# Banded attention: five units turned by VectorE and DMAs instead of TensorE

## The reference, cut to what matters

```python
def window_attention(q, k, v, sink):      # 8 heads, 2 groups of 4 heads share k and v
    scores = einsum('bnqgrd,bnkgd->bngrqk', qb, kb) * HEAD_DIM ** -0.5   # per block of 128
    scores = where(mask, scores + bias, -inf)      # three neighbouring key blocks, |t-s| <= 128
    m = maximum(max(scores, -1), sink)
    p = exp(scores - m)
    probs = p / (sum(p, -1) + exp(sink - m))
    out = einsum('bngrqk,bnkgd->bnqgrd', probs, vb)
ya = window_attention(...) * silu(ga)
```

## Time and profile before

| what | before |
|---|---|
| median of 3 runs | 610.73 us (609.9 to 611.62) |
| profiled execution | 610.19 us, span 608.4 us |
| granted clock of TensorE, mean | 0.997 |
| TensorE busy | 597.4 us, 98% |
| VectorE, ScalarE, GpSimd busy | 446.7, 357.1, 293.3 us |

### The profile page before, as it was taken

One profiled execution on the slowest core, in us unless ns is written; L12 is line 12 of the kernel. 1 busy time (PEld: TensorE's weight loads), 2 busy tenths in 40 slices (PEclk: granted clock), 3 DMA queues, 4 the chain that ended last, 5 costly groups with the idle time before them and its releaser, 6 DMA issues.

```text
span 608.4 us, 9184 instructions
## 1 busy us (share of the span) xinstructions
PE 597.4 (98%) x3076; PEld 482.6 (79%) x3076; DVE 446.7 (73%) x802; ACT 357.1 (59%) x762; POOL 293.3 (48%) x273
## 2 busy tenths in 40 slices
PE   8999999999999999999999999999999999999996
PEld 7888888888888888888887777767776777888885
DVE  4776753334434439889999788988998988799884
ACT  5644243213333238777886777878887789534563
POOL 4510704315756432536537545876876766510601
PEclk9999999999999999999999999999999999999998
DMA  6688458674876620101015967767767745598042
GB/s 222 207 256 245 146 163 266 202 270 135 256 263 233 201 67 1 36 1 36 2 27 137 250 150 183 188 165 194 194 161 195 183 133 182 176 387 319 1 170 108
DMA packets 72431, 102.11 MB, mean 168 GB/s; under 512 B 10232, under 2 KB 43008, under 8 KB 72384
## 3 DMA queue, kind: packets, MB, share of 16 engines
q1 hardware_dynamic: 72224, 101.25, 55.7%
q10 hardware_dynamic: 160, 0.27, 0.1%
HBM read 60.17 MB, written 31.62 MB: 151 GB/s over the span
## 4 chain that ended last, share of the span: by engine, by line
PE 78%; DMA 7%; DVE 5%; ACT 4%; SPq 3%; POOL 2%; issue 1%; ACTq 0%
PE ps L1821 18%; PE ps L1823 18%; PE ps L1822 18%; PE ps L2093 4%; DMA p_land<-probs_scratch 4%; PE ps L1993 3%; PE ps L2112 2%; PE ps L2113 2%; PE ps L2023 2%; SPq L628 2%; PE ps L2003 2%; DMA probs_scratch<-p_blk 2%; PE ps L2028 2%; PE ps L1980 2%; PE ps L1979 2%; DVE pT_lo L1671 2%
## 5 line engine op out<-in xcount | busy, mean ns | idle before, releaser
L1671 DVE TENSOR_TENSOR pT_lo<-ps,pT_hi 128x512 fp32r<-128x512 f32 x102 | 68.8, 688 | 25.0 <-ACT pT_hi L1234 24.9
L1821 PE MATMUL ps<-hT_hi,w_hi 128*128 128x512 f32 x208 | 84.0, 404 | 0.0
L1221 ACT ACTIVATE p_b<-ps,stat 128x1024 f32<-128x1024 f32 x64 | 71.4, 1116 | 19.2 <-DVE stat L1646 18.9
L1823 PE MATMUL ps<-hT_hi,w_lo 128*128 128x512 f32 x208 | 81.3, 391 | 0.0
L1822 PE MATMUL ps<-hT_lo,w_hi 128*128 128x512 f32 x208 | 81.0, 389 | 0.0
L1646 DVE TENSOR_REDUCE stat<-ps 128x1 f32<-128x1024 f32 x64 | 76.6, 1215 | 2.2 <-PE ps L2043 2.0
L1234 ACT ACTIVATE pT_hi<-ps 128x512 fp32r<-128x512 f32 x102 | 60.0, 596 | 18.8 <-PE ps L2093 18.5
L2093 PEld LDWEIGHTS ps<-ident,p_b 128*128 128x128 f32 x408 | 47.9, 140 | 19.6 <-DVE pT_lo L1671 5.4
L2093 PE MATMUL ps<-ident,p_b 128*128 128x128 f32 x408 | 62.6, 276 | 0.5 <-DVE pT_lo L1671 0.3
L2112 PE MATMUL ps<-pT_hi,vB 128*128 128x512 f32 x128 | 54.8, 428 | 1.5 <-POOL pT_lo L925 1.5
L809 POOL TENSOR_SCALAR p_w<-p_w,stat 128x384 f32<-128x384 f32 (+1 forms) x40 | 24.4, 623 | 55.5 <-DVE stat L1554 55.5
(11 more groups left out here) (222 smaller groups left out, 1487.7 us busy)
## 6 DMA issues: line engine op xcount, KB each, us to landing
w_raw<-w_in SPq DMA_DIRECT2D x13, 512.0 KB, 4.3
probs_scratch<-p_blk SPq DMA_DIRECT2D x52, 128.0 KB, 2.8
p_land<-probs_scratch SPq DMA_DIRECT2D x13, 512.0 KB, 4.6
x_in<-x SPq DMA_DIRECT2D x8, 512.0 KB, 4.1
wt_raw<-w_out SPq DMA_DIRECT2D x8, 512.0 KB, 4.5
t_scratch<-wt_hi SPq DMA_DIRECT2D x16, 256.0 KB, 2.5
t_scratch<-wt_lo SPq DMA_DIRECT2D x16, 256.0 KB, 2.8
q<-q_h SPq DMA_DIRECT2D x16, 256.0 KB, 3.6
```

The source lines that it names most:

```text
L1221: nc.scalar.activation(p_b[:, (U + 1) % 4, :], ps[:, b:b + 2, :].rearrange("p b c -> p (b c)"), ACT.Exp, bias=nm_b[:, U % 4:U % 4 + 1], ac ...
L1671: nc.vector.tensor_tensor(pT_lo[at_], ps[:, 4 + a, :].rearrange("p (k c) -> p k c", c=P), f(pT_hi[at_]), ALU.subtract).then_inc(s_bTl, 1)
L1821: nc.tensor.matmul(o, a_hi, b_hi, start=first, stop=False, skip_group_check=goes_on)
L1823: return nc.tensor.matmul(o, a_lo, b_hi, start=False, stop=last, skip_group_check=goes_on)
```

## The change

Units 5, 7, 9, 11 and 13, all with g = 1 and three key blocks, take the way through DRAM. After GpSimd has multiplied all four heads of such a unit, VectorE turns 32x32 blocks of all 1536 columns in step u+1 into `w_blk`, four stores of 192 KB and one load of 768 KB follow on SyncE's queue, and in step u+3 ScalarE copies the high part from `w_land`, GpSimd subtracts (three times, one per key block) and TensorE multiplies with the values. Both strips lie in parts of `q_st` whose queries are done. The other units stay as they were. So step 6 has no products, steps 8, 10, 12 and 14 have those of units 5, 7, 9 and 11 and no transposes, step 16 has those of 13 ahead of 15. The gated groups are dealt out anew: 2 and 6 in steps 5 and 6, then 3 in odd and 5 in even steps up to 14.

The diff, cut to its core (semaphore counts that shift by the number of routed units are left out):

```diff
+W_ROUTED = [5, 7, 9, 11, 13]
+POOL_HEADS = [3, 2, 2] + [2 if u in ACT_UNITS else 4 if u in W_ROUTED else 3 for u in range(3, 16)]
+        w_strips = at("w_strips", 65, [P, 4, 2, SEQ])
@@ beside
+            cut = 2 if s in (5, 6) else 3 if 7 <= s <= 14 else 4
+            return N_WIN_JOB + (s + 1) // 2, range(cut) if s % 2 else range(cut, KT)
+        def w_now(s):
+            return [u for u in (s - 3, s - 1) if 0 <= u < W_UNITS and (u in W_ROUTED) == (u == s - 3)]
+        w_blk, w_land = (w_strips[:, :, i, 0:3 * P] for i in range(2))
@@ SyncE
+            def store_w_probs(u):
+                i = W_ROUTED.index(u)
+                sp.wait_ge(s_pblk, NT + i + 1)
+                for q in range(4):
+                    sp.dma_start(pw_scr[i % 2, :, :, q, :].rearrange("a p c -> p a c"),
+                                 w_blk[q * Q32:(q + 1) * Q32]).then_inc(s_psto, 16)
+            def fetch_w_probs(u):
+                i = W_ROUTED.index(u)
+                sp.wait_ge(s_psto, 64 * (NT + i + 1))
+                if i >= 1:
+                    sp.wait_ge(s_plo, NT + 3 * i)
+                sp.dma_start(w_land, pw_scr[i % 2].rearrange("a p q c -> (a p) q c")).then_inc(s_pin, 16)
+            store_w_probs(5)
+            fetch_w_probs(5)
             sp.wait_ge(s_wr, NM - 1)
...
             load_k(0)
+            for u in (7, 9, 11):
+                store_w_probs(u)
+                fetch_w_probs(u)
             sp.wait_ge(s_wr, NM)
             load_q(0)
+            store_w_probs(13)
+            fetch_w_probs(13)
@@ GpSimd
+            def routed_w_lo(u, i):
+                c = W_FIRST[u] + i
+                pool.wait_ge(s_wTh, c + 1)
+                nc.gpsimd.tensor_tensor(w_quads_out(pT_wl[:, c % 2, :]), w_quads(i), w_quads_out(f(pT_wh[:, c % 2, :])),
+                                        ALU.subtract).then_inc(s_plo, 1)
@@ head0_hi
+                pool.wait_ge(s_psto, 64 * (NT + WR))
                 nc.gpsimd.tensor_scalar(k_1[:, 0, :], k_raw[:, :], 1.0, 1.0, ALU.mult, ALU.mult).then_inc(s_h0kh, 1)
@@ its loop over steps
+                for u in w_now(s):
+                    if u in W_ROUTED:
+                        for i in range(3):
+                            routed_w_lo(u, i)
                 if s < W_UNITS:
                     probs_w(s)
-                if s >= 2:
-                    gate_w(s - 2)
+                for u in w_now(s - 1):
+                    gate_w(u)
@@ ScalarE, pT_w_hi
+                if u in W_ROUTED:
+                    act.wait_ge(s_pin, 16 * (NT // 2 + W_ROUTED.index(u) + 1))
...
+                    nc.scalar.activation(w_quads_out(pT_wh[:, c % 2, :]), w_quads(i), ACT.Copy).then_inc(s_wTh, 1)
@@ VectorE
+            def turn_w_probs(u):
+                i = W_ROUTED.index(u)
+                dve.wait_ge(s_wp, sum(POOL_HEADS[:u + 1]))
+                dve.wait_ge(s_ws, REP * 6)
+                if i >= 1:
+                    dve.wait_ge(s_psto, 64 * (NT + i))
+                nc.vector.transpose(w_blk.rearrange("p a (k c) -> p a k c", c=Q32),
+                                    p_w[:, u % 2, :, :].rearrange("p r (i a c) -> p a (r i) c", a=4, c=Q32)) \
+                    .then_inc(s_pblk, 1)
@@ its loop over steps, ahead of recip_w(s)
+                if s - 1 in W_ROUTED:
+                    turn_w_probs(s - 1)
@@ TensorE, pv_w
-                pe.wait_ge(s_wTl, c + 1)
+                if u in W_ROUTED:
+                    pe.wait_ge(s_plo, NT + 3 * W_ROUTED.index(u) + i + 1)
+                else:
+                    pe.wait_ge(s_wTl, W_TURN[u] + i + 1)
@@ its loop over steps
+                for v in now[:-1]:
+                    pv_w(v, 0)
+                    gated(g, ks[:1])
+                    pv_w(v, 1)
+                    gated(g, ks[1:2])
+                    pv_w(v, 2)
+                    ks = ks[2:]
+                if u not in W_ROUTED:
+                    for i in range(min(n, 2)):
+                        turn_w(u, i)
```

More of the change, by code:

```diff
@@ L66 @@
 ACT_UNITS = range(2, 16, 2)
-POOL_HEADS = [3, 2, 2] + [2 if u in ACT_UNITS else 3 for u in range(3, 16)]
+W_ROUTED = [5, 7, 9, 11, 13]
+WR = len(W_ROUTED)
+POOL_HEADS = [3, 2, 2] + [2 if u in ACT_UNITS else 4 if u in W_ROUTED else 3 for u in range(3, 16)]
 SLOPE = [2.0 ** -(h + 1) for h in range(HEADS)]
@@ L1179, in _ @@
             for s in range(W_UNITS + 1):
-                keys = range(W_FIRST[s - 1], W_FIRST[s]) if s >= 1 else []
+                now = w_now(s)
+                keys = [(now[-1], i) for i in range(len(w_keys(now[-1])))] if now else []
                 live = s < W_UNITS
-                if s >= 2:
-                    o_w_lo(s - 2)
+                for u in w_now(s - 1):
+                    o_w_lo(u)
+                for u in now[:-1]:
+                    for i in range(len(w_keys(u))):
+                        pT_w_hi(u, i)
                 if live:
@@ L1187, in _ @@
                     first_v_hi()
+                for u in now[:-1]:
+                    o_w_lo(u)
                 for i, c in enumerate(keys[:2]):
-                    pT_w_hi(c)
+                    pT_w_hi(*c)
                     if live:
@@ L1556, in probs_w @@
             def probs_w(u):
+                if POOL_HEADS[u] == REP:
+                    return
                 dve.wait_ge(s_wrd, u + 1)
@@ L1606, in _ @@
             for s in range(W_UNITS + 1):
-                keys = range(W_FIRST[s - 1], W_FIRST[s]) if s >= 1 else []
+                now = w_now(s)
+                keys = [(u, i) for u in now if u not in W_ROUTED for i in range(len(w_keys(u)))]
                 live = s < W_UNITS
@@ L1616, in _ @@
                     head0_lo()
-                if s >= 1:
-                    pT_w_lo(keys[0])
+                for u in now[:-1]:
+                    o_w_sum(u)
+                for c in keys[:1]:
+                    pT_w_lo(*c)
                 if live:
@@ L1983, in turn_w @@
             def turn_w(u, i):
-                c = W_FIRST[u] + i
+                c = W_TURN[u] + i
                 if i == 0:
                     pe.wait_ge(s_wp, sum(POOL_HEADS[:u + 1]))
-                    pe.wait_ge(s_wpd, u + 1)
+                    pe.wait_ge(s_wpd, sum(v not in W_ROUTED for v in range(u + 1)))
                     if u in ACT_UNITS:
@@ L2050, in _ @@
                 g, ks = beside(s)
[L2051 removed]
+                now = w_now(s)
+                u = now[-1] if now else None
+                n = len(w_keys(u)) if now else 0
                 if s < W_UNITS:
                     scores_w(s)
[L2054 to L2058 removed]
+                for v in now[:-1]:
[8 more added lines that the diff above has]
+                        turn_w(u, i)
                 if 2 <= s < W_UNITS or s == 0:
```

109 lines of the change are left out of this document (60 added, 49 removed).

## The result

| | before | after |
|---|---|---|
| median | 611.17 us (609.9 to 612.16, 4 runs) | 630.03 us (629.8 to 631.15, 4 runs) |
| ratio | | 1.0328, interval 1.0297 to 1.0359 |
| profiled span | 608.4 us | 628.0 us |
| granted clock, mean | 0.997 | 0.986 |
| TensorE busy, matmuls | 597.4 us, 3076 | 598.4 us, 3016 |

The changed kernel takes 630.03 us, 3.3% more than before, where 632 us were forecast. TensorE has 60 matmuls less and is busy no less, since some of them run at half clock. First the page of the profile after: busy time by engine, then TensorE and its granted clock in 40 slices. They answer to the earlier trace rows.

A forecast was written before the change was run, and what follows sets the result against it. TensorE, busy 98% of the span, was taken as the bound. Even steps 9.3, steps 6 and 7 -0.2, step 16 8.0 and clock 4.4 gave 21.5 us more, so 632 us, range 619 to 641.

The forecast's parts named there:

- Removed transposes: TensorE, five routed units: 1.37 us less work per unit, 6.8 us in all, the most that can be won.
- rival 1: Window stage: transposes are won and all waits covered, 604 us; chance 4%.
- Even steps: Steps 8, 10, 12, 14: TensorE waits for GpSimd's queued subtractions; longer by 2.7, 2.4, 3.4, 0.8, together 9.3 us.
- Odd steps and steps 6 and 7: Odd steps stay at 7.17 us on VectorE's chain; steps 6 and 7 together win 0.2 us.
- Step 16: End of window stage: TensorE waits 5.9 us for unit 13's subtraction, last in GpSimd's queue; head 0 starts 8.0 us later.
- The transfers: Strips through DRAM: 10 us taken from end of turn to ScalarE's copy, covered, so costed at nothing.
- The clock: TensorE's clock falls in four stalls of 3.3, 3.0, 4.0 and 5.9 us: 1.1 us each, 4.4 together.
- Rival 2: Window stage: the clock doesn't fall in the stalls, 627.8 us; chance 25%.
- Rival 4: The low clock holds to the end of each stalled step, 15.0 us, giving 643 us; chance 10%.
- Rival 3: Splits on GpSimd come earlier, so only step 16 and 0.8 us per even step count, 621.7 us; chance 12%.
- Rival 5: Strips land late, 12.9 us for 10 to 12: up to 1 to 3 us per unit, 636 us; chance 6%.

The follow-up runs named there:

- e4: Kernel before with 45 of the 60 transposes of the five units left out, nothing in their place (output not the reference's); 606.92 us, 0.9961.
- e6: Changed kernel with unit 13's subtractions earlier, second and third weight splits and k_c split one step later, routed units' first product behind three gated groups; 621.39 us.
- e3: Changed kernel with idle identity transposes on TensorE filling the stalls of steps 12 (34) and 16 (50); 628.17 us, 1.0296.
- e2: Changed kernel with GpSimd's two weight splits and the k_c split one step later, behind the subtractions; 625.19 us, 1.0234.
- e5: Changed kernel with the fourth head of the routed units moved back from GpSimd to VectorE; 627.62 us, 1.0295.
- e1: Changed kernel with unit 13's three GpSimd subtractions ahead of the gate product and the second half of head 0's k; 628.53 us, 1.0295.
- e7: Changed kernel with unit 13 back on TensorE's transposes, splits one step later, first routed product behind three gated groups; 623.6 us, 1.0244.

## Why the prediction was right

**Removed transposes.** The prediction took 6.8 us as the most that could be won; nothing on record comes near that bound. In the kernel before, e4 shows 0.33 to 0.42 us per even step for nine transposes, since VectorE's low part is next behind TensorE there. In the changed kernel that low part is GpSimd's, and no run shows what it would win with every wait covered; in the best order, e6, the first product of step 8 comes 4.6 us into the step, where rival 1 (604 us) needed its low part at 2.78.

**Even steps.** Forecast +2.7, +2.4, +3.4, +0.8 for steps 8, 10, 12, 14. Steps 8, 10 and 14: +2.46, +2.19, +0.73. Step 12: +5.96, of which e3 gives the clock 2.8, so 3.2 without it. Step 14 fits by luck in part: the prediction has 7.65 us for 6.86, measured are 7.17 for 6.44. Unit 14 has two key blocks, its scores take 0.94 us instead of 1.40, and both kernels have that, so it drops out of the difference. Shown by e2 (splits) and e5 (fourth head) as GpSimd's queue. GpSimd's subtraction, bounded by 0.69 and 1.71 us and taken as 1.29, is 1.28:

```profile
L871 POOL TENSOR_TENSOR pT_wl<-w_strips,pT_wh 128x512 fp32r<-128x512 f32 x15 | 19.0, 1278 | 3.6 <-ACT pT_wh L1209 3.6
...
L1643 DVE STREAM_TRANSPOSE w_strips<-p_w 128x1536 f32<-128x1536 f32 x5 | 8.8, 1768 | 0.0
```

**Odd steps and steps 6 and 7.** Odd steps stayed at 7.15 to 7.17. Steps 6 and 7 gave 0.73, not 0.2: step 7's scores came at 5.5 us, where the prediction let them wait to 6.7, and step 7 then took 7.8 us, not 7.17. VectorE was less late than the prediction added up.

**Step 16.** +9.73; e3, with the clock up, gives +8.35 against the 8.0 forecast. The stall was 5.83 (forecast 5.9). The order of GpSimd's queue was the first reason, but e1 shows that it is worth 1.8 us of the stall and 1.3 us of the time, since the strips land 9.5 us after the turn and are next.

**The transfers.** From the end of unit 5's turn (264.41) to ScalarE's copy (274.71) are 10.3 us, of unit 13's 10.0; forecast 10. The prediction said it would be wrong if ScalarE waited for w_strips to land. It did, 0.63 us for unit 5 and 2.01 us for unit 13, and that cost nothing, because GpSimd's split stood behind it in step 8 and its head 0 work in step 16. The cost at nothing was right for this kernel only; e2 and e6 pay for it.

```profile
274.71 0.63 ACT L1209 ACTIVATE pT_wh<-w_strips 128x512 fp32r<-128x512 f32 x1 [0.63 <-DMA w_strips<-w_probs_scratch]
...
339.96 1.15 ACT L1209 ACTIVATE pT_wh<-w_strips 128x512 fp32r<-128x512 f32 x2 [2.01 <-DMA w_strips<-w_probs_scratch]
```

**The clock.** Forecast four falls of 1.1 us, 4.4 in all; in the trace two falls, 2.8 and 1.4 by e3, 4.2. The sum fits by luck, by two errors that cancel: a fall was mis-sized (in step 12 more than twice as much) and mis-counted. Rival 2 (no fall) is wrong; it is what e3's two filled steps show, 4.2 us less. Rival 4 (low level to the end of each step, 15.0 us) is wrong as a sum: two of its four steps kept the full level, and in step 16 it came back 4.1 us after TensorE went on, 4.2 us before head 0. For step 12 alone it was near: the level came back 6.0 us after TensorE went on, 0.3 us before the step's end, at a price of 2.8 us where the rival has 3.45. The Trainium skill (TensorE: Matmul & The Clock Gate, on HAM oscillation) has waits between short pieces of work putting the engine back to half clock each time. The traces agree in part, since of the twelve stalls of 2.1 to 2.9 us in the window stage five had it, and all ten of 3.06 us and more.

**The sum.** 9.3 - 0.2 + 8.0 + 4.4 = 21.5 was forecast; by steps it is 8.6 (without the clock) - 0.7 + 8.3 + 4.2 = 20.4, read directly 20.3. The spans differ by 19.6, 0.7 less, which lies behind the window stage and within what that part varies by.

**The other rivals.** Rival 3 (621.7 us, splits early enough) needed GpSimd free by 2.65 us into the step; the rows of step 12 show the split without a gap behind heads and gate. It is what e2 and e6 make by hand, at 625.19 and 621.39 us. Rival 5 (strips late, 12.9 us) didn't occur in the change itself, where they were there after 10.3 us at the latest in the two cases in which ScalarE waited; in e2 those of unit 7 took 12.8.

## What to carry to other kernels

An engine that is busy half of the time is no free engine: look at what stands in its queue at the moment when the new work is wanted, above all long side work that nothing waited for until now. What TensorE is spared counts only down to the next engine's chain in that step; leave the work out once, as a probe, before building a way round it. And when a cover is taken away from a wait, the next one behind it (here the landing of the strips) must be priced too. Side work that is moved also meets new neighbours: GpSimd's split, moved by a step, held up a small operation of VectorE and with it a step that was in order before.

## What the runs showed of the hardware

The same idle time of TensorE does not always have the same effect on its clock. Step 8, with equal work before it and 2.84 to 2.88 us of idle, kept the full level in three traces (after twice, e1) and lost it in a fourth (e3), where it fell only after matmuls had begun again; step 10, at 2.59 to 2.61 us, likewise. A thirteenth stall of this size, 2.99 us in e2 and ahead of the window stage, kept the full level too:

```profile
99.69 0.50 PE L1911 MATMUL ps<-latT_hi,uq_hi 128*128 128x512 f32 x1 [2.99 <-DVE latT_lo L1473]
...
98.00:100.00 2.00, 0.31 (x1) 1.00 1.01 368
100.00:102.00 2.00, 2.00 (x10) 1.00 0.92 307
```

What decides between them is open.

A low stretch lasted 3.4 us in six of the fifteen falls and 6.8 us in nine, and nothing in between, after stalls of 2.35 to 3.06 us in the six and of 3.56 to 5.83 us in the nine. It began 1.8 to 3.9 us after TensorE had run dry. So the price is at most half of what part of it falls on work: 1.6 us for a short one in e3 (eight matmuls at 0.43 us spacing), 2.8 and 1.4 us for the two long ones in steps 12 and 16. In e1 a stall of 4.00 us was followed by 12 slow matmuls, in the changed kernel one of 5.83 us by 9, since in the longer stall more of the low stretch passed in idle.

VectorE's small operations can wait for GpSimd. One of 128x4 (lines 1617 and 1623 of the changed kernel) took 0.12 to 0.27 us by itself. Where it met a long GpSimd instruction, a weight split or a low part above all, it took up to 1.35 us and ended with that instruction, within 0.04 us:

```profile
307.51 2.35 POOL L795 TENSOR_TENSOR w_lo<-w_raw,w_hi 128x1024 fp32r<-128x1024 f32 x1
...
308.54 1.34 DVE L1617 TENSOR_TENSOR stat<-stat,nsink 128x4 f32<-128x4 f32 x1
```

The kernel before has one such case in the window stage, the changed one nine. There they cost TensorE nothing that the step lengths show; in steps 9 and 13 of e2, e6 and e7 they cost some 0.5 us each.
